# An expert stage reordered: selection before the block list, an early first window, a residual that stays in PSUM, and the put-back between gate and up

## The reference, cut to what matters

```python
h2 = rms_norm_3(x, norm_ffn_w, 1e-6)
x  = x + hierarchical_moe(h2, ...)          # 64 experts in 8 groups, top 2 within the best group
return rms_norm_3(x, final_norm_w, 1e-6)

# inside hierarchical_moe, t = h2 as 256 rows of 1024
g_sel = argmax(t @ w_gr + b_gr)             # the group
e_sel_logits = (t @ w_er + b_er) of that group
top_v, top_i = top_k(e_sel_logits, 2)
weights = g_gate * softmax(top_v)
# each expert, for its tokens in blocks:
hid = silu(x_blk @ w_gate[e]) * (x_blk @ w_up[e])      # 1024 -> 512
out[token] += weight * (hid @ w_down[e])                # 512 -> 1024
```

## Time and profile before

| what | value |
|---|---|
| median of 3 runs | 2837.94 us (2836.89 to 2840.13) |
| the profiled execution's own time | 2836.18 us |
| its span, first to last instruction | 2834.4 us |
| mean granted TensorE clock | 0.992 of 2.4 GHz |
| first expert block's gate product begins | 2205.53 us |
| first load that waited for a used piece | 2209.39 us |
| last block's gate product begins | 2808.28 us |

### The profile page before, as it was taken

One profiled execution on the slowest core, in us unless ns is written; L12 is line 12 of the kernel. 1 busy time (PEld: TensorE's weight loads), 2 busy tenths in 40 slices (PEclk: granted clock), 3 DMA queues, 4 the chain that ended last, 5 costly groups with the idle time before them and its releaser, 6 DMA issues. The chain is left out here.

```text
span 2834.4 us, 44443 instructions
## 1 busy us (share of the span) xinstructions
PE 2708.1 (96%) x18750; PEld 2280.6 (80%) x18750; DVE 1438.2 (51%) x2805; ACT 515.2 (18%) x1095; POOL 0.2 (0%) x4
## 2 busy tenths in 40 slices
PE   8999899999999999999999999999998898888887
PEld 8998799999988999888988998888896554444443
DVE  7768677687555775544345657365434111111112
ACT  1001410010043100223010012344302111111111
POOL 0000000000000000000000000000000000000000
PEclk9999999999999999999999999899999999999999
DMA  7644145355354453536544444555554899999997
GB/s 232 212 157 156 52 157 179 134 182 176 120 134 149 151 177 116 135 108 156 170 149 149 155 121 107 150 150 133 137 171 182 339 427 426 426 426 426 427 427 332
DMA packets 371212, 589.09 MB, mean 208 GB/s; under 512 B 17104, under 2 KB 328688, under 8 KB 348912
## 3 DMA queue, kind: packets, MB, share of 16 engines
q1 hardware_dynamic: 366256, 582.21, 58.4%
q10 hardware_dynamic: 4800, 4.63, 0.6%
HBM read 585.72 MB, written 1.08 MB: 207 GB/s over the span
## 5 line engine op out<-in xcount | busy, mean ns | idle before, releaser
L844 PE MATMUL bank<-hR,ring 128*128 128x128 f32 x2112 | 267.4, 277 | 3.9 <-DVE hR L426 3.9
L3498 DVE TENSOR_TENSOR wk<-bank,wk 128x256 f32<-128x256 f32 x43 | 26.1, 608 | 466.5 <-PE bank L3421 466.5
L844 PEld LDWEIGHTS bank<-hR,ring 128*128 128x128 f32 x2112 | 252.7, 194 | 4.9 <-DMA ring<-in_ffn_w_in 2.7
L3441 PE MATMUL bank<-ring,wk 128*64 128x512 f32 x688 | 157.1, 598 | 24.1 <-ACT wk L3458 24.1
L3421 PE MATMUL bank<-ring,wk 128*64 128x256 f32 x1344 | 153.0, 381 | 19.6 <-DMA ring<-in_w_expert_up 19.6
L3421 PEld LDWEIGHTS bank<-ring,wk 128*64 128x64 f32 x1344 | 94.3, 137 | 85.3 <-DMA ring<-in_w_expert_up 26.8
L1164 PE MATMUL bank<-big,ring 128*128 128x128 f32 x1320 | 159.6, 275 | 0.0
L1164 PEld LDWEIGHTS bank<-big,ring 128*128 128x128 f32 x1320 | 153.5, 192 | 0.1
L733 PE MATMUL bank<-hR,ring 128*128 128x256 f32 x704 | 152.3, 379 | 0.0
L733 PEld LDWEIGHTS bank<-hR,ring 128*128 128x128 f32 x704 | 133.8, 190 | 18.2
L2272 PE MATMUL bank<-big,ring 128*128 128x256 f32 x640 | 141.2, 379 | 1.5 <-ACT big L2844 1.0
(11 more groups left out here) (495 smaller groups left out, 4619.3 us busy)
## 6 DMA issues: line engine op xcount, KB each, us to landing
ring<-in_ffn_w_in SPq DMA_DIRECT2D x88, 1024.0 KB
ring<-in_w_expert_down SPq DMA_DIRECT2D x43, 2048.0 KB
ring<-in_w_in SPq DMA_DIRECT2D x96, 512.0 KB
ext<-in_w_expert_gate SPq DMA_DIRECT2D x22, 2048.0 KB, 25.6
big<-in_w_expert_up SPq DMA_DIRECT2D x22, 2048.0 KB, 25.8
ring<-in_w_expert_gate SPq DMA_DIRECT2D x21, 2048.0 KB
ring<-in_w_expert_up SPq DMA_DIRECT2D x21, 2048.0 KB
ring<-in_ffn_w_out SPq DMA_DIRECT2D x40, 1024.0 KB
```

What stands on the lines that cost most here:

```text
L844: last = nc.tensor.matmul(k.bank[:, 2 * (n % 4) + p // 4, (p % 4) * P:(p % 4 + 1) * P], a[:, c, m * P:(m + 1) * P], b[:, c, :], start=c == ...
L3441: last = nc.tensor.matmul(k.bank[m * SLOTS:(m + 1) * SLOTS, self.DOWN, :], ht[:, c * SLOTS:(c + 1) * SLOTS], self.piece(h, 2)[:, a:a + 512 ...
L3498: chain(v.tensor_tensor(by_row, up, gate, ALU.mult), self.hid_ready)
```

## The change

In PE's order `gather` moves ahead of the turned list, and `clear` goes. In DVE's order (b) comes first, then (d) with `eid_ready` 1, then (a), then (c), (e), (f); the expert ids are `eid_ready` 2 now and the first places 3. ACT copies the first block's window right after the sorted rows, ahead of `drow` and `wrow`. The turning of x at L578 becomes ordinary 32-bit matmuls with the identity, so that banks 0 to 3 hold x and the puts add to it; the copies at L605, the zeroing and the last additions (L3491) go, and the final norm reads the banks. The put stands between the next block's gate and up product.

```diff
 # TokenNorm.pe
-                    last = nc.tensor.transpose(k.bank[:, 2 * t + b // 2, (c % 4) * P:(c % 4 + 1) * P],
-                                               k.xT[:, c, t * P:(t + 1) * P], k.c("ident"))
+                    last = nc.tensor.matmul(k.bank[:, 2 * t + b // 2, (c % 4) * P:(c % 4 + 1) * P], k.xT[:, c, t * P:(t + 1) * P],
+                                            k.c("ident"), start=c % 4 == 0, stop=True, skip_group_check=True)
 # TokenNorm.act
-        for t in range(T):
-            last = nc.scalar.activation(k.x[:, t, :]..., k.bank[:, 2 * t:2 * t + 2, :], ACT.Copy)
-        last.then_inc(self.xn_ready, 1)
 # FinalNorm.act
-            act.wait_ge(self.experts.x_summed, n + 1)
-            nc.scalar.activation(k.wk[:, n * 512:(n + 1) * 512], self.quarter(k.x, n), ACT.Square, ...
+            act.wait_ge(self.experts.put_done, self.experts.taken * 2 + (n + 1))
+            nc.scalar.activation(k.wk[:, n * 512:(n + 1) * 512], k.bank[:, n, :], ACT.Square, ...
 # Route.pe
+        self.experts.gather(pe)
         pe.wait_ge(self.list_ready, 1)
         nc.tensor.transpose(k.bank[0:1, 4, P:2 * P], k.small[:, 0:1], k.c("ident")).then_inc(self.row_ready, 1)
-        self.experts.clear(pe)
-        self.experts.gather(pe)
         pe.wait_ge(self.list_ready, 2)
         nc.tensor.transpose(k.bank[0:1, 4, 2 * P:3 * P], k.small[:, 2:3], k.c("ident")).then_inc(self.row_ready, 1)
         pe.wait_ge(self.dest_ready, 1)
         ...                                   # L3116, as before
 # Route.act
         self.experts.take_sorted(act)
+        act.wait_ge(self.eid_ready, 1)
+        act.wait_ge(self.experts.xs_taken, KC)
+        self.experts.take_window(act, slice(0, 1)).then_inc(self.experts.xg_ready, 1)
         act.wait_ge(self.row_ready, 3)
 # Route.dve, after rank_ready: first places and selection (b), then
         self.experts.select(chain)
+        of = wk[:, 464:528]
+        for n, oh in enumerate((guess.at(guess.FIRST, 64), second)):
+            tt(of, tokens, oh, ALU.mult)
+            chain(v.tensor_reduce(cols(14 + n, 1), of, AX, ALU.add))
+        chain(v.tensor_copy(k.first[0:1, 0:2], cols(14, 2)[0:1, :]), self.eid_ready)
+        ...                                   # nb, end, big, list_ready 1, rounds: as before
+        dve.wait_ge(self.row_ready, 1)
+        chain(v.tensor_copy(k.eid[0:1, :], k.bank[0:1, 4, P:2 * P]), self.eid_ready)
         first = wk[:, 400:464]
         ...                                   # (c), (e), (f)
 # Experts.pe and block
-        pe.wait_ge(self.route.rows_taken, 2)
-        pe.wait_ge(self.route.eid_ready, 2)
         self.block(pe, None, 1)
         ...
             self.arrived(pe, i, h, j)
+            if i is None and j == 1:
+                pe.wait_ge(self.route.eid_ready, 3)
             ...                               # the gate or up product
             last.then_inc(k.w_used, 1)
-        if i is not None:
-            pe.wait_ge(self.y_taken, self.at_block(i, 1, h, 1))
-            pe.wait_ge(self.gw_ready, self.at_block(i, 1, h, 1))
-            self.put(pe)
+            if i is not None and j == 0:
+                pe.wait_ge(self.y_taken, self.at_block(i, 1, h, 0))
+                pe.wait_ge(self.gw_ready, self.at_block(i, 1, h, 0))
+                self.put(pe)
+        if i is None:
+            pe.wait_ge(self.route.rows_taken, 2)
 # Experts.dve, at the end
-        for j in range(4):
-            dve.wait_ge(self.put_done, n * 2 + (j + 1))
-            quarter(j).then_inc(self.x_summed, 1)
 ...
```

More of the change, by code:

```diff
@@ L646, in act @@
         for n in range(4):
[L647 to L648 removed]
+            act.wait_ge(self.experts.put_done, self.experts.taken * 2 + (n + 1))
+            nc.scalar.activation(k.wk[:, n * 512:(n + 1) * 512], k.bank[:, n, :], ACT.Square, scale=1.0 / 32,
                                  accum_out=k.ss[:, n:n + 1]).then_inc(self.squared, 1)
@@ L667, in scale @@
         x = self.quarter(k.x, n)
-        chain(nc.vector.scalar_tensor_tensor(x, x, k.ss[:, 10 + n // 2:11 + n // 2], k.r(self.row)[:, (n % 2) * 512:(n % 2 + 1) * 512],
+        chain(nc.vector.scalar_tensor_tensor(x, k.bank[:, n, :], k.ss[:, 10 + n // 2:11 + n // 2], k.r(self.row)[:, (n % 2) * 512:(n % 2 + 1) * 512],
                                              ALU.mult, ALU.mult), self.scaled)
@@ L3188, in dve @@
         both, second = guess.at(guess.BOTH, 64), guess.at(guess.SECOND, 64)
[L3189 to L3200, removed]
         def every(row):
@@ L3217, in dve @@
         self.experts.select(chain)
+        of = wk[:, 464:528]
[3 more added lines that the diff above has]
+        chain(v.tensor_copy(k.first[0:1, 0:2], cols(14, 2)[0:1, :]), self.eid_ready)
+        nb, end, big = wk[:, 600:664], wk[:, 664:728], wk[:, 728:792]
+        chain(v.scalar_tensor_tensor(nb, counts, 0.5, guess.at(guess.NEITHER, 64), ALU.is_gt, ALU.mult))
+        for n in range(1, S // SLOTS):
+            chain(v.scalar_tensor_tensor(nb, counts, n * SLOTS + 0.5, nb, ALU.is_gt, ALU.add))
+        chain(v.tensor_tensor_scan(end, nb, zero, 0.0, ALU.add, ALU.add))
+        chain(v.tensor_scalar(big, end, k.c("row"), None, ALU.is_le))
+        chain(v.tensor_reduce(cols(1, 1), big, AX, ALU.add))
+        chain(v.tensor_scalar(cols(0, 1), cols(1, 1), float(NEXP - 1), None, ALU.min), self.list_ready)
+        chain(v.tensor_copy(k.rounds[0:1, 0:1], end[0:1, NEXP - 1:NEXP]))
+        chain(v.tensor_single_scalar(k.rounds[0:1, 1:2], k.rounds[0:1, 0:1], 1, ALU.logical_shift_right))
+        chain(v.tensor_single_scalar(k.rounds[0:1, 2:3], k.rounds[0:1, 1:2], 1, ALU.add))
+        dve.wait_ge(self.row_ready, 1)
+        chain(v.tensor_copy(k.eid[0:1, :], k.bank[0:1, 4, P:2 * P]), self.eid_ready)
         first = wk[:, 400:464]
@@ L3233, in dve @@
         chain(v.tensor_scalar(cols(2, 1), cols(2, 1), float(2 * S), None, ALU.min), self.list_ready)
[L3234 to L3237, removed]
         base, shift = wk[:, 200:264], wk[:, 320:384]
@@ L3354, in sp @@
                 self.load(sp, sp.value_load(k.eid[0:1, bass.ds(i * 2 + (1 + h), 1)], min_val=0, max_val=NEXP - 1), i, h)
[L3356 to L3364, removed]
     def gather(self, pe):
@@ L3443, in block, with take_window @@
         last.then_inc(k.w_used, 1)
+    def take_window(self, act, index):
+        first = act.value_load(self.k.first[0:1, index], min_val=0, max_val=2 * S)
+        return self.k.nc.scalar.activation(self.window(), self.sorted_rows()[:, :, bass.ds(first, SLOTS)], ACT.Copy)
     def act(self, act, chain):
         k, nc = self.k, self.k.nc
-        def take_window(index):
-            first = act.value_load(k.first[0:1, index], min_val=0, max_val=2 * S)
-            return nc.scalar.activation(self.window(), self.sorted_rows()[:, :, bass.ds(first, SLOTS)], ACT.Copy)
         def block(i, h):
@@ L3460, in block @@
             nc.scalar.activation(self.w(self.Y, 512), k.bank[:, self.DOWN, :], ACT.Copy).then_inc(self.y_taken, 1)
-        act.wait_ge(self.route.eid_ready, 2)
-        take_window(slice(0, 1)).then_inc(self.xg_ready, 1)
+        act.wait_ge(self.route.eid_ready, 3)
         block(None, 1)
-        with act.Fori(0, self.rounds(act)) as i:
+        n = self.taken = self.rounds(act)
+        with act.Fori(0, n) as i:
             for h in range(2):
                 block(i, h)
-    def empty(self, chain):
-        chain(self.k.nc.vector.memset(self.w(self.Y, 512), 0.0), self.y_taken)
-        chain(self.k.nc.vector.memset(self.w(self.GW, S), 0.0), self.gw_ready)
     def select(self, chain):
@@ L3514, in dve @@
         chain.leave(n)
-        for j in range(4):
-            dve.wait_ge(self.put_done, n * 2 + (j + 1))
-            quarter(j).then_inc(self.x_summed, 1)
-            if j == 2:
-                chain.sem = self.tail_chain
-                self.final.variance(dve, chain, 0)
+        chain.sem = self.tail_chain
+        self.final.variance(dve, chain, 0)
 def first_block(k):
```

16 lines of the change are left out of this document (4 added, 12 removed).

## The result

The changed kernel takes 2843.73 us (median of 18 runs, 2840.04 to 2845.09) beside 2837.35 us for the kernel before (18 runs). The ratio is 1.0023, 95% interval 1.0017 to 1.0029: slower by 6.4 us, where 2844.1 was forecast. Two runs stood far off all others, 3193.81 us in e5 and 5396.51 us of the kernel before beside e5 to e8, and no ratio counts them.

What follows compares the result with a forecast made beforehand. Bound: the stream of expert-weight loads, started by the first gate product's end. Terms 1.64 + 5.3 (first load) + 0.1 - 0.4 - 0.5 = +6.1 us gave 2842.3, by the median 2844.1; forecast 2842.3 to 2847.8 (0.70), range 2839.8 to 2847.6.

Steps and rivals of the forecast that it cites:

- Term c: Gather on PE: starts at 1.2 GHz after an idle stretch and loses time until the clock is back, +2.2 us.
- f: First block's gate product: part of it runs at 1.2 GHz until the clock rises, +0.5 us.
- i: Final norm: ACT squares the banks without the addition before it, so the first square comes sooner, -0.5 us.
- Term g: Ramp of the expert stage: PE's block becomes 14.2 us, still under the stream's 14.76; cost +0.1 us.
- Term d: Behind the gather: list turned only then, so DVE's 7.68 us of ids, slots and weights no longer run beside it.
- term e: Slots' products (L3116) on PE: run at the low clock after a pause, 3.4 us instead of 2.04.
- Term b: DVE's selection put ahead of the list: the gather can start 2.89 us sooner.
- Term a: Turning of x before the router projection: 32 matmul records instead of 16 on the path, +1.64 us.
- h: Last block: with the put between gate and up, the down product starts sooner, -0.4 us.
- E: First gate product runs right behind gather and window, first load 4.1 us sooner: 2834.7 us; chance 0.04.
- R: In the ramp, places freed later make the stream stand at three loads: +2.5, 2846.6 us; chance 0.10.
- M: Turning x by matmuls costs four times, 5.1 us instead of 1.64: 2847.6 us; chance 0.04.

Runs made afterwards that it cites:

- e5: Changed kernel with the turned first places and the spreading of slots and weights moved behind the first block's gate product on PE: 2838.87 us, ratio 1.0007.
- e8: Kernel of e7 with the put moved back behind the up product: 2829.39 us, ratio 0.9973.
- e1: Changed kernel with the block list turned on PE inside the gather, after its second of eight parts, not behind it: 2834.82 us, ratio 0.9989.
- e4: Changed kernel with the list made and turned ahead of the selection again, on DVE and PE: 2838.52 us, ratio 1.0004.
- e7: Kernel of e6 with three unread products added on PE ahead of the gather to keep it busy: 2830.71 us, ratio 0.9977.
- e2: Kernel before, with only x turned by 16 ordinary matmuls instead of 16 transposes: 2839.97 us, ratio 1.0012.
- e6: Kernel of e1 with x turned behind the router projection and the sum of squares on PE: 2832.14 us, ratio 0.9983.
- e3: Changed kernel with the put back behind the up product: 2844.38 us, ratio 1.0023.

## Why the prediction was right

The forecast was 2844.1 with the change slower by 6.1; measured are 6.4 by the times and 5.6 by the stretches of one pair of executions. The runs confirm its mechanism, and show one term behind it to be wrong. The closeness of the total is in part luck: against the table the forecast is 0.8 too high in c, 0.5 in f and 0.3 in i, and 0.8 too low in g. With the mean cost of the clock in c (2.3 us, below) the other three cancel. The instants that it named came out sooner than forecast, the gather by 1.8, L3111 by 2.6 and the first load by 2.9 us, of which 1.8 is the early start of this execution.

*Term d, the list behind the gather* (7.1 us forecast, 7.1 in the table): shown. The ids are released by the turned list, the wait is 11.9 us long as forecast, and e1, which undoes only this, gives 8.7 us back. It is more than 7.1 because the pause that lowered the clock for L3111 goes with it (term e): from the slots' products to the gate product it is 1.95 us in e1 instead of 3.59.

*Term b, selecting first* (-2.9; -3.0): shown by the table, and by e1 against e4.

*Term c, the clock* (+2.2; +1.4 here, 2.3 on the mean of six): shown by the gathers of e7 and e8. The size was right as a mean; this execution came out 0.9 below it, by luck. That 0.9 is about what lies between the 5.6 of the stretches and the 6.4 of the times; that it comes from there is argued, not shown.

*Term a, the turning of x* (+1.64; +1.8): shown by e2. But I had the transposes on the path of the kernel before. e6 shows that there DVE's step on x held the projection just as long (1.6 us either way): the transposes only filled that wait, and what cost time was the part of the matmuls beyond it. Behind the projection they cost nothing: from the projection to the gather it is 19.0 us in e6 and 19.8 in e1.

*Terms e and f*: the slots' products took 3.6 us at the low clock, where 3.4 was forecast. PE's rest before them was not the single pause of over 7 us that I took, but 3.56 and 4.00 with the turned first places (L3105) in between, which my working left out; the clock fell all the same. The gate product lost nothing, because the clock was back by 2209 to 2210; in e2, e3 and e5 it took 5.36, 4.29 and 5.32 us instead of 3.67 and so lost 1.7, 0.6 and 1.7.

*Term g failed.* I had put a block at PE's pace at 14.2 us (the terms given add up to 14.25), well under the stream's 14.76, and concluded that PE waits for pieces again late in the stage. A block takes 14.42 us. The timeline of PE in the changed kernel, early in the stage:

```profile
2227.29 3.67 PE L3408 MATMUL bank<-ring,wk 128*64 128x256 f32 x32
...
2232.77 3.65 PE L3430 MATMUL bank<-ring,wk 128*64 128x512 f32 x16 [0.66 <-ACT wk L3447]
2236.25 3.63 PE L3408 MATMUL bank<-ext,wk 128*64 128x256 f32 x32
2239.81 1.99 PE L3380 MATMUL bank<-wk 64*128 64x512 f32 x8
2241.72 3.67 PE L3408 MATMUL bank<-big,wk 128*64 128x256 f32 x32
...
2247.19 3.65 PE L3430 MATMUL bank<-ring,wk 128*64 128x512 f32 x16 [0.65 <-ACT wk L3447]
```

From down to down it is 3.48 (down) + 3.56 (gate) + 1.91 (put) + 5.47 (up to down) = 14.42. What was mis-sized is above all the last: I took 5.35 from the first block. In the loop ACT's copy of the next window (L3436), which stands ahead of its copy of the turned hidden rows, begins 4.42 us after the up product and not 4.31 as in the first block (2818.59 to 2823.01 against 2213.01 to 2217.32). In the code the first block reads its window's place at a fixed address and the loop at a computed one; that this is the reason is argued, not shown. Over 41 blocks the 0.2 is some 7 to 9 us. With a block of 14.2 PE would have used up the lead of the first pieces; at 14.42 it just doesn't, and the last gate product comes 0.9 us behind where the stream of the kernel before would have put it (2213.37 + 598.89 = 2812.26 against 2813.12). By the stream of e2 (599.88) it would be a tie. PE is still faster than the stream by 0.34 us a block (14.76 less 14.42), so by an estimate from these numbers at most three more blocks would use up the lead and make it wait for pieces again. Terms h and i came out as -0.3 and -0.8, and 0.5 of the latter is the earlier first square (1.37 us behind the last put instead of 1.88).

*The rivals.* W (the clock holds) is excluded by the two falls in the windows. E (the first tokens come sooner) is the one that e5 builds: it is worth some 4 us, but only when PE's order is changed, as the prediction said. It gives no more, because the up product waits for the slots. R (the stream starves) didn't happen: the loads move at 406 to 434 GB/s in windows of 4 and 5 us between 2216 and 2240, the kernel before at 393 to 442, and at 424 to 427 later. M is excluded by e2's stretch. S (the stream's pace moves) is excluded: the rate is the same at either pace.

## What to carry to other kernels

When work is moved ahead in two engines' orders, draw each cross-engine wait in both: an item that is ready early but stands behind a long run in its engine's queue makes its reader stand for all of it. A short product that others wait for goes inside the long run, not behind it (e1, 8.7 us for the place of two lines). And work that hides nothing but an idle stretch may still be holding the clock: before removing it, look at what the next long product will run at.

## What the runs showed that I had not expected

A pause of 3.04 us on PE before the gate product left the granted clock at 1.00 in the kernel before. One of 3.05 let it fall within 2206 to 2207 in e2, and one of only 2.26 in e5 (0.54 in the window 2204 to 2205), each at a cost of 1.7 us. So the length of the pause alone doesn't tell the clock. Where PE has just rested, executions of the same code on the same data differ by 1 to 2 us: after, e3 and e5 are alike up to the gather, and it took 15.4, 16.9 and 16.6 us.

The pace of the stage changed hands from the stream to PE with no change in the rate of the loads, which stayed at 426 GB/s in both. The chain, the missing waits for pieces and the steadiness of the stretch (599.75 to 599.79) told who set it.
